# Two transformer blocks on one core: the last two modulation units of each first-block layer move from VectorE to GpSimd

## The reference

```python
c_act = jax.nn.silu(c)
for l in range(DEPTH):
    mod = c_act @ w_ada[l] + b_ada[l]                      # 1024 -> 6 * 1024
    shift1, scale1, gate1, shift2, scale2, gate2 = jnp.split(mod, 6, axis=-1)
    hdn = modulate(rmsnorm(x, norm1_g[l]), shift1, scale1)
    ...                                                    # w_in, three attentions
    merged = (g_a * (o_mla @ w_o_mla[l]) + g_b * (o_sb @ w_o_sb[l])
              + g_c * (o_mb @ w_o_moba[l]))
    x = x + gate1[:, None, :] * (merged @ w_out[l])
    hdn = modulate(rmsnorm(x, norm2_g[l]), shift2, scale2)
    ff = jnp.square(jax.nn.relu(hdn @ w_ff1[l])) @ w_ff2[l]
    x = x + gate2[:, None, :] * ff
```

## Time and profile before

| | us |
|---|---|
| median of 3 runs | 1732.49 |
| lowest, highest | 1729.63, 1732.66 |
| the profiled execution, its own time | 1734.68 |
| its span, first to last instruction | 1732.9 |
| TensorE busy | 1668.6 (96%) |
| VectorE busy | 1188.0 (69%) |
| ScalarE busy | 838.7 (48%) |
| GpSimd busy | 142.5 (8%) |
| mean share of the 16 DMA engines, ring's queue | 57.2% |

### The profile page before, as it was taken

How to read it: one execution, slowest core, us unless ns; L and a number is a source line. 1 busy time by engine, 2 the same in 40 slices (tenths; PEclk the granted TensorE clock), 3 DMA queues, 4 the chain that set the end, 5 groups by cost and what they waited for, 6 DMA issues and landing times.

```text
span 1732.9 us, 24804 instructions
## 1 busy us (share of the span) xinstructions
PE 1668.6 (96%) x9283; PEld 1369.4 (79%) x9283; DVE 1188.0 (69%) x2052; ACT 838.7 (48%) x1460; POOL 142.5 (8%) x297
## 2 busy tenths in 40 slices
PE   7999999999999999999999999989999999899998
PEld 3887775689878786774799878767998787579986
DVE  5777655866766875656735675676788756767885
ACT  3354453455443442642455344475555544755542
POOL 0210101000000000220000000051000000510000
PEclk8999999999999999999999999999999999999999
DMA  9887435557855975336466656704665567046652
GB/s 345 284 281 260 142 98 167 184 194 249 300 167 167 353 250 189 122 98 207 134 211 202 193 164 202 208 2 142 208 185 184 156 215 202 1 153 201 183 185 82
DMA packets 185912, 323.71 MB, mean 187 GB/s; under 512 B 13540, under 2 KB 101184, under 8 KB 185792
## 3 DMA queue, kind: packets, MB, share of 16 engines
q1 hardware_dynamic: 183200, 320.54, 57.2%
q10 hardware_dynamic: 2592, 1.57, 0.3%
HBM read 321.02 MB, written 1.05 MB: 186 GB/s over the span
## 4 chain that ended last, share of the span: by engine, by line
PE 69%; DVE 17%; ACT 6%; DMA 3%; issue 3%; POOL 1%; SPq 0%; DVEq 0%; POOLq 0%; ACTq 0%
PE bank L747 67%; DVE ring_r L1835 6%; PE bank L756 3%; DMA ring<-in_w_in 2%; ACT sm L1468 2%; DVE ada L1947 1%; ACT high L1382 1%; DVE sm L2027 1%; DVE gates_r L1860 1%; DMA ring<-in_w_ada 1%; POOL sm L673 1%; DVE oT L1911 0%; DVE gates L2528 0%; DVE oT_r L1867 0%; DVE pT L2059 0%
## 5 line engine op out<-in xcount | busy, mean ns | idle before, releaser
L1835 DVE TENSOR_TENSOR ring_r<-ring,high 128x1024 fp32r<-128x1024 f32 (+3 forms) x390 | 461.2, 1198 | 267.9 <-ACT high L1382 260.0
L1382 ACT ACTIVATE high<-ring 128x1024 fp32r<-128x1024 f32 (+3 forms) x390 | 401.9, 1037 | 483.5 <-PE bank L747 354.0
L747 PE MATMUL bank<-ring_r,featT_r 128*128 128x512 f32 (+3 forms) x928 | 355.5, 383 | 0.0
L747 PE MATMUL bank<-high,featT_r 128*128 128x512 f32 (+3 forms) x712 | 277.1, 389 | 9.9 <-DVE ring_r L1835 3.0
L747 PE MATMUL bank<-featT_r,high 128*128 128x256 f32 x960 | 272.7, 284 | 0.0
L747 PE MATMUL bank<-featT_r,ring_r 128*128 128x256 f32 x960 | 271.6, 283 | 0.0
L747 PE MATMUL bank<-oT_r,high 128*128 128x256 f32 x960 | 271.6, 283 | 0.0
L747 PE MATMUL bank<-high,oT_r 128*128 128x512 f32 (+3 forms) x712 | 270.8, 380 | 0.0
L747 PE MATMUL bank<-high,gates_r 128*128 128x512 f32 x736 | 230.1, 390 | 3.4 <-DVE ring_r L1835 2.6
L747 PEld LDWEIGHTS bank<-ring_r,featT_r 128*128 128x128 f32 x928 | 175.7, 189 | 27.1 <-issue 0.5
L747 PEld LDWEIGHTS bank<-featT_r,high 128*128 128x128 f32 x960 | 184.2, 192 | 0.8 <-DVE ring_r L1835 0.5
(11 more groups left out here) (271 smaller groups left out, 2147.3 us busy)
## 6 DMA issues: line engine op xcount, KB each, us to landing
ring<-in_w_ff SPq DMA_DIRECT2D x128, 512.0 KB, 4.7
ring<-in_w_ada SPq DMA_DIRECT2D x96, 512.0 KB, 5.8
ring<-in_w_up SPq DMA_DIRECT2D x176, 256.0 KB, 3.4
ring<-in_w_in SPq DMA_DIRECT2D x64, 464.0 KB, 5.2
ring<-in_w_in SPq DMA_DIRECT2D x48, 512.0 KB, 5.5
ring<-in_w_in SPq DMA_DIRECT2D x48, 474.0 KB, 4.8
ring<-in_w_down SPq DMA_DIRECT2D x44, 512.0 KB, 3.4
ring<-in_w_out SPq DMA_DIRECT2D x24, 512.0 KB, 4.8
```

Source lines behind the costliest of these rows:

```text
L747: ins = pe.matmul(o, a, b, start=start, stop=stop, skip_group_check=True)
L1382: act.activation(it["high"], it["raw"], ACT.Copy).then_inc(high_ready, 1)
L1835: dve.tensor_tensor(it["low"], it["raw"], it["high"].bitcast(F32), ALU.subtract).then_inc(low_ready, 1)
```

## The change

A second accumulator `ada_late` (three rows of 512 columns: two units and one for products) and two semaphores are added. The eight `w_ada` pieces of units 10 and 11 of a layer are read by GpSimd (`late_step`), right behind its last softmax scaling of that layer. [...] The ring slots of these pieces now come free by `late_used`. TensorE's `modulation(10)` and VectorE's `modulation_out(l, 10)` move from the projections into unit 1 of `w_ff1`, directly ahead of those of unit 11.

```diff
+        ada_late = sb("ada_late", [P, 3, 512])
...
-            ada_of_layer = ada_order(l, 10, 12)
+            ada_of_layer = ada_order(l, 10, 12, "pool")
...
                     for _ in range(2 if br < 2 else 0):
-                        ada_piece()
+                        late_piece()
...
-        used_by = {"pe": piece_used, "dve": ada_used}
+        used_by = {"pe": piece_used, "dve": ada_used, "pool": late_used}
...
+            def late_step():
+
+                n, it = next(late_steps)
+                acc = ada_late[:, n // 4 % 2, :]
+                if n >= 8 and n % 8 == 0:
+                    pool.wait_ge(part_ready, PARTS1 * (n // 8))
+                pool.wait_ge(w_loaded[it["slot"]], it["loaded"])
+                for kk in range(2):
+                    c = 2 * (n % 4) + kk
+                    row, by = it["raw"][:, kk, :], c_act[:, c:c + 1]
+                    if c == 0:
+                        link(pool.tensor_scalar(acc, row, by, None, ALU.mult))
+                    else:
+                        link(pool.tensor_scalar(ada_late[:, 2, :], row, by, None, ALU.mult))
+                        link(pool.tensor_tensor(acc, acc, ada_late[:, 2, :], ALU.add))
+                pool.sem_inc(late_used, 1)
+                if n % 4 == 3:
+                    pool.sem_inc(late_ready, 1)
...
                 softmax_heads(moba_jobs)
+                for _ in range(8):
+                    late_step()
                 rstd_parts(IN_TURN)
...
-                seen.more(ada_ready)
-                acc = ada[:, u % 2, :]
+                seen.more(late_ready if u >= 10 else ada_ready)
+                acc = (ada_late if u >= 10 else ada)[:, u % 2, :]
...
                         linear((for_dve, for_dve), lambda c, t: out_of(4 * br + c)[:, t, :])
-                        if br and u == 0:
-                            modulation(10)
...
                     if u in FF_OUT[l]:
+                        if u == 1:
+                            modulation(10)
                         modulation(FF_OUT[l][u][1])
...
                             read(r, dve.tensor_tensor(dst, b[:, :], g, ALU.mult))
-                            if t:
-                                ada_step()
-                                ada_step()
                             continue
...
                         link(dve.tensor_tensor(dst, dst, tm, ALU.add))
-                        if br == 1 and t:
-                            ada_step()
-                            ada_step()
-                            if hf == 0:
-                                modulation_out(l, 10)
...
                     if u in FF_OUT[l]:
+                        if u == 1:
+                            modulation_out(l, 10)
                         modulation_out(*FF_OUT[l][u])
```

More of the change, by code:

```diff
@@ L274, in two_blocks @@
         c_ready = sem("c_ready")
-        ada_used = sem("ada_used")
-        ada_ready = sem("ada_ready")
+        ada_used, late_used = sem("ada_used"), sem("late_used")
+        ada_ready, late_ready = sem("ada_ready"), sem("late_ready")
         row_out = sem("row_out")
@@ L341, in cols_piece @@
             return piece(k1 - k0, at, parts, reader, split)
-        uses = {"pe": 0, "dve": 0}
+        uses = {"pe": 0, "dve": 0, "pool": 0}
         def used(it):
@@ L376, in plain @@
                 put(it)
-        ada_pieces = []
+        ada_pieces, late_pieces = [], []
         def ada_piece():
@@ L382, in ada_piece, with late_piece @@
             ada_pieces.append(it)
+            put(it)
+        def late_piece():
+            it = next(ada_of_layer)
+            late_pieces.append(it)
             put(it)
@@ L410, in split_together, with ada_order @@
                 it["q"] = len(split_pieces) - 8 + n
-        def ada_order(l, first, last):
+        def ada_order(l, first, last, reader="dve"):
             for u in range(first, last):
                 for k0 in range(0, KD, 2):
-                    yield cols_piece(w_ada[l], k0, k0 + 2, (512 * u, 512 * u + 512), reader="dve")
+                    yield cols_piece(w_ada[l], k0, k0 + 2, (512 * u, 512 * u + 512), reader=reader)
         IN_STEPS = [[2] * 10, [0, 4, 4, 4] + [2] * 6]
@@ L674, in softmax_heads @@
                     ins.then_inc(p_ready, 1)
+            late_steps = iter(enumerate(late_pieces))
+            def late_step():
[15 more added lines that the diff above has]
+                    pool.sem_inc(late_ready, 1)
             def diagonal(view, told):
```

## The result

The changed kernel is slower: a median of 1739.24 us (1736.37 to 1743.6, 7 runs) against 1732.66 of the kernel before in the same comparison; ratio 1.0043, 95% interval 1.0029 to 1.0057. The ratios are computed from all executions and are not the quotients of the two medians (1.0038 and 1.0057). The forecast was 1729.7, with a range from 1727.6 to 1733.6. The profiled execution took 1738.51 us, with a span of 1736.8.

What follows compares the result with a forecast made beforehand. TensorE was taken as the bound, busy 96% of the span, with gaps hanging on a VectorE chain headed by the last two `ada_step`. Per layer -1.4 us, together -2.8 from 1732.49, gave 1729.7; range 1727.6 to 1733.6.

Steps and rivals of the forecast that it cites:

- The bound on GpSimd's product: GpSimd's product on 512 columns: between a memset's 0.53 us and the sum's 1.11, taken as 0.70.
- the sum: Forecast total per layer: -1.17 - 0.2 - 0.86 + 0.86 = -1.4 us; both layers -2.8 us.
- the sentence that SyncE passes its list: SyncE's load list: the same loads, no wait met later; second `w_out` piece issued at 302.4 instead of 303.29.
- A step: GpSimd's work per `w_ada` piece: two products, two sums and four links, 4.0 us, between 3.6 and 4.8.
- The removed work: Projections, per layer: VectorE loses 16 `ada` instructions, some 12 us, and TensorE one matmul of ones, 0.86 us.
- the gaps: TensorE's idle times ahead of the tile 0 and tile 1 transposes, 2.9 us over both layers; both were to close.
- The second gap: TensorE's 0.29 us idle ahead of the tile 1 transposes; closes with 0.2 us to spare, counted as 0.2.
- The rival on the other side: GpSimd stands in VectorE's way: 1737, or up to 1750 if slow steps also make `w_out` late; chance 0.11.
- The matmul of ones: Moved from the projections to unit 1 of `w_ff1`, where TensorE is busy: minus 0.86, plus 0.86 us per layer.
- The landing of `w_out`: First two `w_out` pieces, issued at 300.7 and 302.4, 0.9 us earlier, have high parts done at 307.3 and 308.7.
- rival 2: The gaps stay: `w_out` may land as late as before and head VectorE's chain; worth 0 to -1.2, 1731.9; chance 0.14.
- the first gap: TensorE's 1.17 us idle ahead of the tile 0 transposes; closes with 1.7 us of slack.

Runs made afterwards that it cites:

- e1: Changed kernel with each GpSimd product written with two operations, (row * c) * 1.0, instead of one; 1729.18 us against 1731.63 for the kernel before, ratio 0.9984.
- e7: Changed kernel with GpSimd only waiting for the pieces and freeing them, plus one memset per unit; 1728.44 us, ratio 0.9984 to the kernel before.
- e4: Kernel before with VectorE's last two `ada_step` of each layer emptied of arithmetic, still waiting and freeing the slot; 1729.48 us against 1731.63, ratio 0.9988.
- e5: Kernel before with VectorE's eight steps of units 10 and 11 moved earlier into its own idle time, GpSimd unused; 1729.96 us against 1731.73, ratio 0.9991.
- e2: Changed kernel with GpSimd's instructions reading a constant tile and VectorE freeing the pieces where it did before; 1734.64 us against 1731.63, ratio 1.0017.
- e9: Changed kernel with GpSimd products and sums replaced by memsets sized to free the pieces as late, reading nothing; 1735.09 us against 1731.73, ratio 1.0019.
- e10: Changed kernel with the GpSimd products' scalar a constant in the instruction instead of a tile column; one run, 1739.98 us.
- e3: Changed kernel with each GpSimd product and sum replaced by three memsets, too narrow to hold the slots as long; 1730.08 us, ratio 0.9990 to the kernel before.

## Why the prediction was wrong

**The bound on GpSimd's product failed, and with it the sum.** The prediction took 0.70 us, "not above the sum's 1.11 us". Measured: 1.56. The sum was a little short too, 1.11 for 1.27. With the step fell the sentence that SyncE passes its list "with the waits met earlier, none later": the second piece of `w_out` was issued 5.2 us later than before, and VectorE waited 3.96 us for its high part. The rows did hold a warning. The product was bounded by a memset and by a two-input sum of another line, both other operations. But the earlier trace rows have a `tensor_scalar` with one operation (L693, a constant added) at 0.38 us on 64 columns; two-operation ones of the same shape in that trace (L691) took 0.25. Half as much again on 64 columns is over twice as much on 512. A bound from another operation is no bound. The Trainium skill, "GPSIMD Engine Reference", section "Elementwise — side-by-side cycle accounting", gives a body of up to two operations 1.03 cycles an element, which would be 0.44 us for 512 elements at its 1.2 GHz, as an estimate, before the start of the instruction. The two-operation form (0.69) lies 0.25 us above that; the one-operation form (1.56) does not fit it, and the measurement decides.

A step was therefore 2 x 1.56 + 2 x 1.27 and gaps, some 6 us, outside the 3.6 to 4.8 given.

**The removed work was priced rightly.** With the product cheap (e1: -2.5 us), absent (e7: -3.3) or the VectorE steps alone emptied (e4: -2.2), the gaps close as worked out and the time falls by about the 2.8 us of the forecast. The second gap did not close as worked out: 0.18 to 0.29 us of it stayed in e1, e4, e5 and e7, where the sum had counted 0.2 of 0.29 as gone. In e1 and e4 the transposes of tile 1 nevertheless came 6.04 us after those of tile 0, for 6.50 before; in e5 it was 6.46. So that the total came out near 2.8 is in part luck.

**The rival on the other side was the right one, with too small a chance (0.11).** It named both the port and, above 5.3 us a step, the late `w_out`. In its details it was partly off. It had the eighth slot and the sixth piece of `w_out` as the late ones; what came first was the sixth slot and the second piece, at 308.4 for 302.4. That was in reach: by the prediction's own positions the sixth slot was due near 297, some 5 us ahead of its need, and at its upper bound of 4.8 us a step only 0.7 ahead. Its price, +5 to +9 per layer, was too high for what happened, about +3.5. For the port it had 5.5 us of waits in VectorE's chain and +2.5 per layer; e2 shows 3.0 us of waits and +1.5.

**The matmul of ones** moved at par, 0.86 for 0.86, as forecast.

**Left out:** the clock. That the longer gap costs more than itself, here 1.0 us in layer 0, had no term. The earlier trace rows could not show it: the longest gap there is 1.17 us, and the clock behind it was 1.00.

**What each part costs:** over the kernel before, late slots alone are 3.4 us (e9) and the port 3.0 (e2, with its later landing); over the cap (e7, 3.3 us faster than before) 3.3 us more each. The changed kernel has both, 6.6 to 9.8. e2 and e9 are not exact halves: e2 has the landing in it, e9 a stretch of low clock in layer 1 (below), and both also spend what the removed `ada_step` had won.

**The landing of `w_out`** was expected earlier by as much as its issue (rival 2 had doubts). In e5 the first piece was issued at 300.22, before at 301.60, and used at 307.85, before at 307.10. An earlier issue did not bring it earlier; the slack of the first gap took it.

## What to carry to other kernels

Work given to an engine off the critical path still holds what it reads: look first at which buffers it frees, who loads into them next, and by when. Bound a new instruction by rows of the same operation and the same form, also short ones, and where only one form has been seen, measure the other. And before work is moved to another engine, see whether the first has idle time a few instructions earlier: e5 touches one engine only and wins nearly as much as e1, the fastest here that leaves nothing out (1.8 us beside 2.5, with intervals that overlap).

## What the runs showed of the hardware

- A GpSimd `tensor_scalar` on 128x512 fp32 took 1.56 us with one operation and 0.69 with two (e1). The one-operation form took 1.49 with its scalar in the instruction instead of SBUF (e10).
- GpSimd and VectorE hold each other up in both directions where both read SBUF: a VectorE low part took 1.77 us for 0.68 (e2), a GpSimd product 2.32 for 1.56 (the changed kernel). VectorE's products of a PSUM bank and a tile kept 0.68 to 0.69 us in all runs, and its sums 0.69 beside GpSimd's memsets (e3, e9). The Trainium skill, "SBUF — State Buffer", section "Who interferes with whom", says just this of two SBUF inputs against a GpSimd read, and that a GpSimd instruction that only writes is no hindrance; the traces agree.
- TensorE's granted clock after a gap was 1.00 after 1.17, 1.74 and 2.48 us of idling (the kernel before; e2 and e9, layer 0), and 0.54 after 3.80 us in the changed kernel. After 2.74 us in e9's layer 1 it was 0.52 from 818.7 to 821.2, and the transposes took 1.91 us for 1.06:

```profile
818.75 1.91 PE L790 MATMUL bank<-cst,wide 128*128 128x128 f32 x8 [2.74 <-issue]
```
